# One array of sums in place of two in an attention and mixture-of-experts layer, and another order of its last stage

## The chip, the cores and the metric

The kernel runs on one core of one Trainium2 chip. The metric is the device time of one execution in microseconds (us). A core has TensorE (PE in the profile, with its weight loads as PEld), VectorE (DVE), ScalarE (ACT), GpSimd (POOL) and SyncE (SP), which here only issues DMAs. POOL issues the DMAs whose rows are chosen by an index list, and those that add to memory.

## The reference

One layer with 1024 tokens of 1024 values, all in float32: attention with a forget gate (16 heads), a first LayerNorm, then a mixture of experts and a second LayerNorm.

```python
x = layer_norm(ALPHA * x + fox_mixer(x), ln1_g, ln1_b)
scores = sigmoid(x @ w_router)                  # 64 experts in 8 groups
top_e = the 8 best of the 4 best groups         # per token
w = scores[top_e] / sum * 2.5
y = sum over the 8: (silu(x @ w_gate[e]) * (x @ w_up[e])) @ w_down[e] * w[e]
y = y + (silu(x @ ws_gate) * (x @ ws_up)) @ ws_down      # shared expert, all tokens
out = layer_norm(ALPHA * x + y, ln2_g, ln2_b)
```

The change touches only how the parts of `ALPHA * x + y` are summed, and how the second LayerNorm is staged.

## The kernel before

Tokens stand in TT = 8 tiles of P = 128 rows. Attention runs until some 560 us, the first LayerNorm and the routing until about 700 us, the shared expert (eight blocks, one for each tile) until about 770 us, and the 64 experts until about 1595 us. Then comes the end stage.

**Experts.** A table in memory lists the tokens of each expert. The first 128 of them are the expert's first rows; what is left over goes in blocks of XR = 32 further rows. With this input 31 experts have one such block, and the others none. Weights arrive by SP's DMAs two experts ahead, ACT and DVE split them into a high and a low part, and TensorE multiplies. Rows are gathered by `gather` (L657) and `gather_further` (L670) on POOL. The results lie in `ys[0]` and `ys[1]` for first rows, by the expert's parity, and in `ys[2]` for further rows. ACT writes `ys` out of the PSUM pair `k_ps` in `scale_rows` (L1434), once the add that read this buffer has landed (`sent`).

**Sums.** There are two arrays in memory. `sums[0]` gets the shared expert's rows by a plain store (L711, L749), and to it `add_first` (L673, its DMA L682) adds the first rows of each expert. `sums[1]` gets ALPHA times x by a plain store (L477), and to it `add_further` (L685, its DMA L692) adds the further rows. A token may be in any two experts, so two adds to one array may not overlap, save those of one expert. That is why each add waits for the one before: `add_first` waits for both `sent[par]` and `sent[1 - par]`, and `add_further` waits for `sent[2]`. The two chains don't wait for each other. On POOL all of this is one stream, in this order for each expert e in `expert` (L720): gather the first rows of e + 3, add the further rows of e - 1, gather further rows of e + 1 or e + 2, add the first rows of e - 1.

**The end stage.** The last expert's rows are not added in memory. DVE builds matrices of zeros and ones, `place_of` and `x_place`, and TensorE in `put_in_place` (L1106) multiplies them with the expert's results (high and low part), so that these land at their tokens: four matmuls for the first rows and four for the further rows for each tile, in turn in two pairs of banks, `q_ps` and `k_ps`. A pair is free for tile t when DVE has summed tile t - 2 (`f_mean`). The sums of the other experts come back by `load_sums` (L560): `sums[1]` into `fin1` and `sums[0]` into `fin0`, 8 tiles of 512 KB each. The tiles 0 and 1 of `sums[1]` are loaded ahead of the last adds (after `summed`), the other 14 loads when the last first add has landed (L570). POOL adds the two (L776) and so makes `fin0`; `LAST_POOL` (L77) is its order of work. For each tile then

- DVE adds the bank pair to `fin0` and sums it (L2106), makes the mean (L2115) and multiplies by g2, which lies in `out_ps` (L2120);
- ACT makes the square and the root (L1601, L1603);
- for the tiles 0 to 3 (BIAS_TILES = 4), ACT scales (L1607) and POOL adds the bias b2 (L780); for the tiles 4 to 7 DVE does both in one (L2126), with b2 in `bank_pair`, where ACT copied it (L1585);
- SP stores the tile (L581), in order of tiles.

## Time and profile before

| what | us |
|---|---|
| median of 3 runs | 1645.97 |
| lowest and highest run | 1644.61, 1650.76 |
| span of the profiled execution | 1640.5 |
| PE busy | 1578.0 (96%) |
| DVE busy | 1182.3 (72%) |
| ACT busy | 1032.5 (63%) |
| POOL busy | 503.7 (31%) |
| end of the last first add in memory | 1598.6 |
| end of DVE's last product | 1635.6 |

The span runs from the first to the last instruction of the profiled execution; the page has no other time for it, and the median of the runs lies 5.5 us above the span. Engine names stand as in the profile. An engine that is idle before an instruction is shown with what released it, in square brackets. The chain that ended last is followed back from the last instruction, at each step to what released it.

### The profile page before, as it was taken

Reading aid. Unit: us, or ns where it says so; the run is one execution under the profiler, and the core shown is the slowest. Engines: PE = TensorE matmul, PEld = TensorE weight load, DVE = VectorE, ACT = ScalarE, POOL = GpSimd, SP = SyncE. Lnnn points to the kernel's source line nnn. Section 1 sums busy time; section 2 is a strip of 40 time slices with the busy share of each in tenths; the row PEclk is TensorE's granted clock in tenths of the full one; section 3 lists DMA queues with packets and bytes.
Section 4 is the critical chain, followed back from the end, with each engine's and each line's share of the span. In section 5 each row is a group of like instructions: output and inputs, shape, how many; then the busy total and the mean of one; then the engine's idle time right before and its main releaser. Section 6 shows DMA issues by size and latency. Waiting matters only on the chain.

```text
span 1640.5 us, 32188 instructions
## 1 busy us (share of the span) xinstructions
PE 1578.0 (96%) x8246; PEld 1310.0 (80%) x8247; DVE 1182.3 (72%) x2036; ACT 1032.5 (63%) x1706; POOL 503.7 (31%) x495
## 2 busy tenths in 40 slices
PE   6999999999999999899999999999999999999986
PEld 6897888888887788778878888888888888888863
DVE  4214777777777788847777787777876787888866
ACT  3214666666666655527677787666776777877854
POOL 0000000000000135432544454543454445454426
PEclk9999999999999999899999999999999999999995
DMA  7223222222123533657999999999999999999987
GB/s 245 91 81 91 72 48 68 58 65 71 45 71 103 170 134 138 227 196 281 337 291 318 305 357 367 326 289 264 334 318 288 274 353 331 342 368 370 367 252 282
DMA packets 161320, 368.63 MB, mean 225 GB/s; under 512 B 53009, under 2 KB 73489, under 8 KB 161265
## 3 DMA queue, kind: packets, MB, share of 16 engines
q1 hardware_dynamic: 136272, 284.21, 49.7%
q0 software_dynamic: 24992, 83.73, 19.7%
q8 instruction: 28, 0.46, 0.1%
q14 instruction: 28, 0.22, 0.0%
HBM read 294.39 MB, written 65.11 MB: 219 GB/s over the span
## 4 chain that ended last, share of the span: by engine, by line
PE 72%; DVE 8%; DMA 8%; issue 5%; ACT 3%; ACTq 2%; POOL 1%; SPq 0%; DVEq 0%; POOLq 0%
PE bank_pair L1025 6%; PE bank_pair L1031 6%; PE bank_pair L1028 6%; DMA sums_scratch<-ys,sidx 5%; PE q_ps L91 4%; PE q_ps L93 4%; PE q_ps L92 4%; PE out_ps L916 4%; PE k_ps L894 4%; PE out_ps L1084 3%; PE out_ps L1085 3%; PE q_ps L1015 3%; PE k_ps L1052 2%; PE k_ps L1053 2%; PE k_ps L1060 2%
## 5 line engine op out<-in xcount | busy, mean ns | idle before, releaser
L1918 DVE TENSOR_TENSOR gu_lo<-raw_gu,gu_hi 128x1024 fp32r<-128x1024 f32 x260 | 306.3, 1220 | 25.5 <-ACT gu_hi L1396 25.5
L1396 ACT CAST gu_hi<-raw_gu 128x1024 fp32r<-128x1024 f32 x260 | 253.2, 1050 | 2.3 <-DMA raw_gu<-in_moe_w_gate_dram 1.5
L1025 PE MATMUL bank_pair<-gu_hi,xb_hi 128*128 128x512 f32 x576 | 233.1, 405 | 5.5 <-DVE gu_lo L1918 4.2
L1028 PE MATMUL bank_pair<-gu_lo,xb_hi 128*128 128x512 f32 x576 | 226.9, 394 | 0.0
L682 POOL DMA_INDIRECT sums_scratch<-ys,sidx x63 | 122.1, 1939 | 148.9 <-DMA sums_scratch<-ys,sidx 116.0
L1918 DVE TENSOR_TENSOR dn_lo<-raw_dn,dn_hi 128x1024 fp32r<-128x1024 f32 x130 | 152.6, 1213 | 2.9 <-ACT dn_hi L1396 2.4
L1031 PE MATMUL bank_pair<-gu_hi,xb_lo 128*128 128x512 f32 x576 | 142.7, 390 | 2.0 <-DVE xb_lo L1922 2.0
L1301 ACT CAST pt_hi<-k_ps 128x512 fp32r<-128x512 f32 (+1 forms) x192 | 85.7, 482 | 75.4 <-PE k_ps L894 74.7
L1025 PEld LDWEIGHTS bank_pair<-gu_hi,xb_hi 128*128 128x128 f32 x576 | 110.1, 191 | 28.8 <-issue 6.4
L613 POOL IOTA e<- 128x64 f32 x1 | 0.2, 185 | 428.8 <-DVE xs L1714 428.8
L1396 ACT CAST dn_hi<-raw_dn 128x1024 fp32r<-128x1024 f32 x130 | 130.0, 1052 | 2.9 <-DMA raw_dn<-in_moe_w_down_dram 2.9
L1031 PEld LDWEIGHTS bank_pair<-gu_hi,xb_lo 128*128 128x128 f32 x576 | 108.0, 188 | 24.8 <-DVE xb_lo L1922 2.4
L1028 PEld LDWEIGHTS bank_pair<-gu_lo,xb_hi 128*128 128x128 f32 x576 | 109.7, 190 | 21.1
L657 POOL DMA_INDIRECT x_rows<-rows_scratch,gidx x64 | 77.4, 1210 | 154.2 <-DVE wcol L1934 122.6
L1692 DVE TENSOR_TENSOR pt_lo<-k_ps,pt_hi 128x512 fp32r<-128x512 f32 (+1 forms) x192 | 100.4, 551 | 27.8 <-ACT pt_hi L1301 27.0
L1052 PE MATMUL k_ps<-dn_hi,ht_hi 128*128 128x512 f32 x288 | 118.4, 411 | 0.0
L1053 PE MATMUL k_ps<-dn_lo,ht_hi 128*128 128x512 f32 x288 | 112.5, 391 | 0.0
L91 PE MATMUL q_ps<-xt_hi,wqk_hi 128*128 128x512 f32 x256 | 109.2, 427 | 0.0
L1290 ACT ACTIVATE probs<-bank_pair,nm 128x512 f32<-128x512 f32 (+3 forms) x128 | 74.7, 586 | 43.2 <-DVE nm L1685 29.7
L1084 PE MATMUL out_ps<-gu_hi,xo 128*128 128x512 f32 x248 | 97.3, 392 | 4.5 <-DVE xo L1938 4.5
L93 PE MATMUL q_ps<-xt_hi,wqk_lo 128*128 128x512 f32 x256 | 100.5, 393 | 0.0
L92 PE MATMUL q_ps<-xt_lo,wqk_hi 128*128 128x512 f32 x256 | 100.3, 392 | 0.0
(306 smaller groups left out, 3973.7 us busy)
## 6 DMA issues: line engine op xcount, KB each, us to landing
raw_gu<-in_moe_w_gate_dram SPq DMA_DIRECT2D x128, 512.0 KB, 6.8
raw_gu<-in_moe_w_up_dram SPq DMA_DIRECT2D x128, 512.0 KB, 8.6
raw_dn<-in_moe_w_down_dram SPq DMA_DIRECT2D x128, 512.0 KB, 8.3
wqk<-in_fox_w_in_dram SPq DMA_DIRECT2D x66, 128.0 KB, 2.5
v_scratch<-v_out SPq DMA_DIRECT2D x32, 256.0 KB, 2.8
va<-v_scratch SPq DMA_DIRECT2D x16, 512.0 KB, 4.7
fin<-sums_scratch SPq DMA_DIRECT2D x16, 512.0 KB, 8.3
xs<-in_x_dram SPq DMA_DIRECT2D x8, 512.0 KB, 7.4
```

The lines of the kernel that those rows point to most:

```text
L91: pe.matmul(out, w_hi, m_hi, start=start, stop=False, skip_group_check=True)
L92: pe.matmul(out, w_hi, m_lo, start=False, stop=False, skip_group_check=True)
L93: return pe.matmul(out, w_lo, m_hi, start=False, stop=stop, skip_group_check=True)
L682: g.indirect_dma_start(out=sums[0], out_offset=bass.IndirectOffsetOnAxis(ap=sidx[par][:, 0:1], axis=0), in_=ys[par][:], in_offset=None, co ...
L1025: i = pe.matmul(o3, xb_hi[s][:, c], g_hi[:, :, c], start=c == 0, stop=False, skip_group_check=True)
L1028: pe.matmul(o3, xb_hi[s][:, c], g_lo[:, :, c], start=False, stop=False, skip_group_check=True)
L1031: i = pe.matmul(o3, xb_lo[s][:, c], g_hi[:, :, c], start=False, stop=c == DC - 1, skip_group_check=True)
L1052: pe.matmul(k_ps[:, r], ht_hi[:, c], d_hi[:, c, r], start=c == 0, stop=False, skip_group_check=True)
L1053: pe.matmul(k_ps[:, r], ht_hi[:, c], d_lo[:, c, r], start=False, stop=False, skip_group_check=True)
L1084: pe.matmul(o3, xo[:, c], g_hi[:, :, c], start=c == 0, stop=False, skip_group_check=True)
L1396: a.copy(hi, raw).then_inc(S[done], 1)
L1918: dve.tensor_tensor(lo, raw, hi, ALU.subtract).then_inc(S[lo_ok], 1)
```

## The change

- There is one array, `sums`. SP stores ALPHA times x to it. The shared expert's rows are added to it by an accumulating DMA (before: stored), after a wait for that store. First and further rows are both added to it.
- Therefore `add_further` has a new wait for the first add before it, ahead of its copy of indices, and `add_first` has a new wait for the further rows of the experts before, behind its waits for first adds. One value more (`xb`) is loaded for each expert. One store of zeros (512 KB) is gone.
- In the end all 8 loads (4 MB) come after the last first add. The additions of pairs on POOL are gone; DVE's sum waits for the tile's load.
- `put_in_place` uses three pairs of banks (`q_ps`, `bank_pair`, `k_ps`). It places the first rows of the tiles 0, 1 and 2, then, when the further rows are ready, those of the same tiles, and then from tile 3 on both for each tile, once DVE has summed tile t - 3.
- b2 stays in SBUF. BIAS_TILES is 6: ACT scales and POOL adds the bias for the tiles 0 to 5, DVE does both for 6 and 7.
- ACT takes a square root once ahead of the tiles, and DVE sets `feps` ahead of them. Some waits between semaphore steps of one engine are added for the case without further rows.

```diff
-BIAS_TILES = TT // 2
-LAST_POOL = [("pair", t) for t in range(5)] + [("bias", 0), ("pair", 5), ("bias", 1), ("pair", 6), ("pair", 7), ("bias", 2), ("bias", 3)]
+BIAS_TILES = TT - 2
...
-        sums = [nc.dram_tensor(f"sums_scratch{i}", (ROWS, D), F32, kind="Internal").ap() for i in range(2)]
+        sums = nc.dram_tensor("sums_scratch", (ROWS, D), F32, kind="Internal").ap()
...
-            for t in range(2):
-                load_sums(1, t)
             for i in range(2):
                 sp.wait_ge(sent[i], 8 * E + SENT_0[i] - 16 * i)
-            for t in range(2):
-                load_sums(0, t)
-            for t in range(2, TT):
-                load_sums(1, t)
-                load_sums(0, t)
+            for t in range(TT):
+                sp.dma_start(fin0[:, t], sums[t * P:(t + 1) * P, :]).then_inc(tile_in[t], 16)
...
-            def add_first(par, e):
+            def add_first(par, e, xb):
...
                 pool.wait_ge(sent[1 - par], 8 * (e + par) + SENT_0[1 - par])
+                pool.wait_ge(sent[2], 16 * xb + SENT_0[2])
                 pool.wait_ge(S["scaled"], SH + e + 1)
...
-            def add_further(e, k, x):
+            def add_further(e, k, x, before_par, before):
+                pool.wait_ge(sent[before_par], before)
                 pool.wait_ge(sent[2], 16 * x + SENT_0[2])
...
-                    pool.dma_start(sums[0][(b - 1) * P:b * P, :], ys[(b - 1) % 2][:]).then_inc(sent[(b - 1) % 2], 16)
+                    pool.wait_ge(S["ax_stored"], 16 * b)
+                    pool.dma_start(sums[(b - 1) * P:b * P, :], ys[(b - 1) % 2][:], accum_op=ALU.add).then_inc(sent[(b - 1) % 2], 16)
...
+                xb = None if pos == "first" else earlier_of(e - 1)
...
-            for what, t in LAST_POOL:
-                if what == "pair":
-                    pool.wait_ge(tile_in[t], 16 * 3)
-                    g.tensor_tensor(fin0[:, t], fin0[:, t], fin1[:, t], ALU.add).then_inc(S["f_pair"], 1)
-                else:
-                    pool.wait_ge(S["c_loads"], 96)
-                    pool.wait_ge(S["f_scaled"], t + 1)
-                    g.tensor_tensor(fin1[:, t], fin1[:, t], b2[:], ALU.add).then_inc(S["f_pair"], 1)
+            pool.wait_ge(S["c_loads"], 96)
+            for t in range(BIAS_TILES):
+                pool.wait_ge(S["f_scaled"], t + 1)
+                g.tensor_tensor(fin1[:, t], fin1[:, t], b2[:], ALU.add).then_inc(S["f_pair"], 1)
...
+                places = (q_ps, bank_pair, k_ps)
...
+                pe.wait_ge(S["place_step"], 2)
+                if further_too:
+                    for t in range(3):
+                        first_rows(t)
+                    pe.wait_ge(S["place_step"], 7)
+                    for t in range(3):
+                        further_rows(t).then_inc(S["f_placed"], 1)
...
+                for t in range(3, TT):
+                    pe.wait_ge(S["f_mean"], 2 * (t - 3) + 1)
+                    i = first_rows(t)
                     if further_too:
+                        i = further_rows(t)
                     i.then_inc(S["f_placed"], 1)
...
                     a.copy(out_ps[:], g2[:]).then_inc(S["y_hi_ok"], 1)
-                    a.copy(bank_pair[:], b2[:]).then_inc(S["y_hi_ok"], 1)
...
+            act.wait_ge(S["f_step"], 1)
+            a.activation(fstd[1][:], feps[:], ACT.Sqrt)
...
-                    dve.wait_ge(S["f_pair"], 1 + LAST_POOL.index(("pair", t)) + 1)
+                    dve.wait_ge(tile_in[t], 16 * 2)
...
-                    dve.tensor_tensor_reduce(out=fin0[:, t], in0=(q_ps, k_ps)[i][:], in1=fin0[:, t], scale=1.0, scalar=0.0, op0=ALU.add,
+                    dve.tensor_tensor_reduce(out=fin0[:, t], in0=(q_ps, bank_pair, k_ps)[t % 3][:], in1=fin0[:, t], scale=1.0, scalar=0.0, op0=ALU.add,
...
-                    dve.scalar_tensor_tensor(out=fin1[:, t - 1], in0=fin1[:, t - 1], scalar=frstd[1 - i][:, 0:1], in1=bank_pair[:], op0=ALU.mult,
+                    dve.scalar_tensor_tensor(out=fin1[:, t - 1], in0=fin1[:, t - 1], scalar=frstd[1 - i][:, 0:1], in1=b2[:], op0=ALU.mult,
```

## Rows read from the trace of the kernel before

**Rows 1.** The page, part 1: busy time of each engine, share of the span, instructions.

```profile
PE 1578.0 (96%) x8246; PEld 1310.0 (80%) x8247; DVE 1182.3 (72%) x2036; ACT 1032.5 (63%) x1706; POOL 503.7 (31%) x495
```

**Rows 2.** The chain that ended last, 1440 to 1606: start us, us, what.

```profile
1501.34 9.86 DMA sums_scratch<-ys,sidx
...
1584.20 7.47 DMA sums_scratch<-ys,sidx
...
1592.45 6.13 DMA sums_scratch<-ys,sidx
1598.60 3.46 DMA fin<-sums_scratch
1602.14 2.35 POOL fin L776
1604.63 1.23 DVE fin L2106
```

**Rows 3.** The timeline of the end stage: start us, us, engine, line, operation [idle before].

```profile
1595.35 0.63 PE L1118 MATMUL q_ps<-y_hi,place_of 128*128 128x512 f32 x1
...
1597.90 0.50 PE L1127 MATMUL q_ps<-yx_hi,x_place 64*128 64x512 f32 x1 [0.73 <-DVE yx_lo L2090]
...
1605.92 0.79 PE L1118 MATMUL q_ps<-y_hi,place_of 128*128 128x512 f32 x1 [4.59 <-DVE fsum L2106]
...
1610.56 1.22 DVE L2106 CUSTOM_DVE_ANT_0 fin<-q_ps,fin 128x1024 f32<-128x1024 f32 x1
...
1612.08 1.28 DVE L2120 SCALAR_TENSOR_TENSOR fin<-fin,fnm,out_ps 128x1024 f32<-128x1024 f32 x1
...
1630.17 1.23 DVE L2106 CUSTOM_DVE_ANT_0 fin<-k_ps,fin 128x1024 f32<-128x1024 f32 x1
...
1631.57 4.35 SPq L581 DMA_DIRECT2D out_dram<-fin  x5
...
1634.28 1.28 DVE L2126 SCALAR_TENSOR_TENSOR fin<-fin,frstd,bank_pair 128x1024 f32<-128x1024 f32 x1
```

**Rows 4.** Windows of the end: us; busy PE, PEld, DVE, ACT, POOL; PEclk, DMA share, GB/s.

```profile
1602.00:1606.00 4.00, 0.08 (x1) 0.08 (x1) 1.39 (x4) 0.00 (x0) 3.86 (x2) 0.72 1.03 418
1606.00:1630.00 24.00, 24.00 (x48) 13.79 (x48) 19.92 (x34) 16.19 (x26) 22.62 (x11) 0.50 0.62 250
```

**Rows 5.** Instructions on the tile `fin` from 1586 to 1598: ns min/median/max, first and last start.

```profile
L561 SPq DMA_DIRECT2D fin<-sums_scratch x2: 337/1030/1723, 1586.9 to 1587.3; - x2
```

**Rows 6.** The chain from 1500 to 1512, behind the landing of one add.

```profile
1511.24 0.05 issue
1511.29 0.04 POOLq L680
```

**Rows 7.** The timeline of POOL: a first add and the further add behind it, twice.

```profile
797.75 1.59 POOL L682 DMA_INDIRECT sums_scratch<-ys,sidx  x1 [1.01 <-POOL sidx L677]
...
804.59 1.40 POOL L692 DMA_INDIRECT sums_scratch<-ys,sidx  x1 [0.97 <-POOL sidx L688]
...
1434.94 2.26 POOL L682 DMA_INDIRECT sums_scratch<-ys,sidx  x1 [2.50 <-DMA sums_scratch<-ys,sidx]
...
1445.24 2.28 POOL L692 DMA_INDIRECT sums_scratch<-ys,sidx  x1 [0.95 <-POOL sidx L688]
```

**Rows 8.** Line L682 alone: landing of the adds issued at 797.75 and at 1434.94.

```profile
DMA to landing us min/median/max: 9.2/9.2/9.2
...
DMA to landing us min/median/max: 9.8/9.8/9.8
```

**Rows 9.** Line L682, all 63 first adds: who waited for them (us, times).

```profile
  ACT ys L1444: 1.2, 1
```

**Rows 10.** Line L749, the shared expert's last store: landing.

```profile
DMA to landing us min/median/max: 9.0/9.0/9.0
```

**Rows 11.** The page, part 5: DVE's subtraction of weights; busy us, mean ns, idle before.

```profile
L1918 DVE TENSOR_TENSOR gu_lo<-raw_gu,gu_hi 128x1024 fp32r<-128x1024 f32 x260 | 306.3, 1220 | 25.5 <-ACT gu_hi L1396 25.5
```

**Rows 12.** The tile `out_dram`: landing of its 8 stores.

```profile
DMA to landing us min/median/max: 2.6/4.3/5.2
```

67 lines of the change are left out of this document (33 added, 34 removed).

## The prediction

> **What bounds the kernel now.** I read the page's table of engines first: TensorE is busy in 96% of the span [rows 1], so up to the last experts whatever leaves TensorE fed costs nothing. Then I read the chain that ended last in order of time, because the change works at the end. It leaves TensorE at 1501.34 us: from there it runs from one add of rows into memory to the next, because each add waits until the one before has landed. There are ten adds, and the last three stand at 1584.20, 1592.45 and its landing at 1598.58 [rows 2]. Only then are the sums loaded (3.46 us to the first tile), then come Pool's addition of two tiles (2.35 us) and the first add-and-sum on DVE at 1604.63 [rows 2]. The third view is the timeline of the end: the first sum of a tile lets TensorE place the third tile at 1605.92, and DVE starts its sum of the eighth tile at 1630.17, which is 24.25 us or six placings later, so some 4.01 us each with the wake-up of DVE in it [rows 3]. DVE alone could go faster. Its sum of tile 2 starts at 1610.56 and its product of that tile ends at 1612.08 + 1.28 = 1613.36, so it needs about 2.84 us for a tile [rows 3]. So after the last add TensorE sets the pace, and the windows say why: from 1606 to 1630 it works without a pause (24.00 of 24.00 us) at a granted clock of 0.50, the level of 1.2 GHz [rows 4].
>
> **The change, part by part.** The sum is made against the profiled span of 1640.5 us. The median of the runs, 1645.97, lies 5.5 us above it, and I carry that over.
>
> *The loads that start early go.* Now two tiles of the second array are loaded at 1586.9 and 1587.3 [rows 5], while the add of 1584.20 is still in flight. That add took 7.47 us and the next 6.13 [rows 2]. I take the difference as the price of the overlap: **-1.3 us** on the chain of adds (bounds 0 and -1.3, because another cause may have slowed that add).
>
> *A further wait in each first add.* It is queued on Pool after the wait for the preceding add, so it stands behind the landing. One wait with the issue slot before it takes 0.05 + 0.04 us there [rows 6]; the new one compares with a loaded count, so its value is worked out first, and I take 0.12. Ten adds make **+1.2 us** (bounds 0.9 and 2.5). What is awaited has landed long before: the further rows of two experts back were issued before the first rows that are awaited anyway.
>
> *The further rows now wait for the first rows of the expert before.* At the first of the 30 further adds, the first add issued at 797.75 [rows 7] takes 9.2 us to land [rows 8], till 806.95, while the further add goes out at 804.59 [rows 7], 2.4 us earlier. At a late one it is 1434.94 + 9.8 = 1444.74 against 1445.24: landed 0.5 us before [rows 7, 8]. Behind the wait still come the copy of the indices and a gap, some 1.25 us together, so the first is late by 3.65 us and the second by 0.75. Done so for all 30, these two are the first and the last of 14 that come out late, by 29 us in sum. Behind the wait Pool has queued the next gather of further rows, the first add and then the next gather. This I cost at nearly nothing while an expert with further rows takes longer than a chain link; the scaling on ACT, which needs a buffer of rows back, waited for an add once in the whole loop, for 1.2 us [rows 9]. In the runs without further rows that cover is thin, so I put **+0.3 us** (bounds 0 and +5). If the cover were gone the 29 us would show.
>
> *The shared rows are added, not written.* Eight stores of 512 KB become accumulating ones. The last is the only one Pool waits for at once, and it took 9.0 us [rows 10]; first adds of the same size took 9.2 and 9.8 [rows 8], so 0 to +1 us on Pool, ahead of a gather that is needed later: **0**. The store of x times alpha is over before (its wait is new and met). The dropped 512 KB of zeros is hidden too.
>
> *No Pool addition before the first sum.* Tile 0 lands at 1598.60 + 3.46 = 1602.06. DVE can begin its sum then, at 1602.14 and not at 1604.63 [rows 2]: **-2.5 us**. That wants tile 0 placed by then. TensorE starts placing at 1595.35 and now stops for the further rows until 1597.90 [rows 3]; in the change it places the first rows of tiles 1 and 2 in this gap. Eight matmuls in 4.01 us are 0.50 each at the lower level, so about 0.25 at the higher; twelve for first rows and then four further ones give tile 0 at 1599.4 to 1603.4. With the clock coming back on the way, as it does now (a matmul took 0.63 us at 1595.35 and 0.50 at 1597.90 [rows 3]), it is in time. The other loads come out of 4 MB where 7 MB had to come after the add, in order, and DVE needs a tile only each 2.8 us.
>
> *Three pairs of banks.* After the first sum five tiles are left to place, not six: **-4.0 us** at the present clock. DVE's need of 2.84 us a tile stays under it.
>
> *The six biases.* Pool's addition of a tile takes 2.35 us [rows 2] and has lost its eight additions of pairs, so it stays under the pace. ACT scales two tiles more, before its last square is due. The last two tiles stay on DVE, as now; their product and bias take 1.28 us [rows 3], now with the bias from SBUF. A subtraction on DVE with both inputs in SBUF takes 1.22 [rows 11], so 0. Thus from DVE's sum of tile 7 to the last product's end stay 1635.56 - 1630.17 = 5.39 us [rows 3]. The Trainium skill has a rule against this edit (SBUF — State Buffer, section "SBUF: two separate sides"): a DVE instruction with both inputs in SBUF and a Pool instruction reading SBUF exclude each other for a whole instruction. No row here shows a collision; by it the last but one product could wait for the rest of Pool's sixth bias, and the end would come up to about 1 us later.
>
> *The stores.* Now five stores start between 1631.57 and the end [rows 3] and share the queue. The last product ends at 1635.56, and 4.9 us later the span ends. The quickest store needed 2.6 us from issue to landing, the median 4.3 [rows 12]. With Pool's sixth bias done well before DVE's seventh, the last three go out some 1.3 us apart: near the quickest row, 3.0 us and some 0.3 around it: **-1.6 us** (bounds 0 and -1.9).
>
> The table of the square root is loaded early; it lay in TensorE's shadow, so 0.
>
> Sum: -1.3 + 1.2 + 0.3 - 2.5 - 4.0 - 1.6 = **-7.9 us**: span 1632.6, time 1645.97 - 7.9 = **1638.1 us**.
>
> **The rivals.** *The clock is full in the end stage.* Now TensorE idles for 4.59 us before 1605.92 [rows 3], the clock falls within that (mean 0.72 from 1602 to 1606), and 24 us of continuous placing do not bring it back [rows 4]. With three tiles placed ahead the pause shrinks to some 1.5 us, and it may not fall. Then DVE paces: the eighth sum starts at 1602.1 + 7 x 2.84 = 1622.0 and not at 1630.17 - 6.5 = 1623.7, so 1.7 us more off: **1636.4**. The Trainium skill would have it so (TensorE: Matmul & The Clock Gate, section "Why this matters for your kernels"): continuous work brings the full clock. By that rule the trace disagrees: 24 us at 0.50. Against the rival speaks also that at the higher level a placing takes 2.0 of DVE's 2.84 us, so TensorE would pause between them. 0.15.
>
> *The clock is low from the first placing on.* Then eight placings of 4.01 us from 1595.35 end at 1627.4, and the eighth sum starts at 1627.6, only 2.6 us earlier than now: -1.3 + 1.2 + 0.3 - 2.6 - 1.6 = -4.0: **1642.0**. Against it: the shorter matmul at 1597.90. 0.10.
>
> *The longer chain of adds reaches TensorE.* Some of Pool's lateness, or late gathers in the last runs without further rows, costs 3 to 7 us of the loop: **1641 to 1645**. 0.12.
>
> *Slower.* The same mechanism in full: each late further add holds the gather and the first add behind it, ACT waits for its buffer and TensorE for ACT, and the 29 us arrive whole: +29 - 8 = +21, **1667**. It turns into a loss when more than 8 of the 29 us get through. Against it: ACT waited only once for an add [rows 9]. 0.07.
>
> *The gain isn't one*: tiles land late or Pool's biases hold the stores, so that only the shorter placing is left: -4, near **1642**, 0.06.
>
> **How the numbers follow.** The forecast has 0.50. Its own range, from the bounds of the adds, stores and the loop, is 1635.5 to 1643. The range of 8 in 10 takes in the full clock, the low clock and the passed-on lateness: **1634.5 to 1645.5**. About 0.5%, or 8.2 us, is what a measurement of this kernel can tell from no change, so the edge is 1637.7, only 0.4 under the forecast. Of the forecast's 0.50 about 0.24 lie below it, and of the full clock's 0.15 about 0.13: **faster 0.38**. The rest of these and the middle cases are **same, 0.55**; the last rival gives **slower, 0.07**.
>
> **What would show it.** In the changed profile: DVE's first sum directly behind tile 0's landing, some 2.5 us sooner after the last add; five placings after it, of 4 us at clock 0.50; the last adds spaced by 7 us with nothing loading beside them; the last store landing in about 3 us; no new idle of TensorE between 780 and 1590 us. I am wrong if the last add lands more than 2 us off 1598.6, if placings take 2 us, or if ACT's scaling waits for adds repeatedly.

## The result, and the profile after

The changed kernel takes 1658.2 us (1651.45 to 1659.7) against 1646.5 for the kernel before in the same rounds: a ratio of 1.0065 (1.004 to 1.0089), which is 10.7 us slower (11.7 by the two medians). The prediction was 1638.1. Timed once more (after_again, below) it was 1.006.

The end stage did what was forecast, and the loop over the experts lost more than that gave back. First the page, part 1, to set beside [rows 1]:

```profile
PE 1584.7 (96%) x8246; PEld 1315.0 (79%) x8247; DVE 1178.8 (71%) x2034; ACT 1034.1 (62%) x1708; POOL 491.2 (30%) x488
```

It shows nothing amiss: TensorE is again at 96%. The chain shows it. Here is the share of each line in the chain that ended last, from 850 to 1600 us, first of the kernel before:

```profile
by line: DMA sums_scratch<-ys,sidx 11.9%; PE bank_pair L1025 9.7%; PE bank_pair L1031 9.7%; PE bank_pair L1028 9.7%; PE out_ps L1084 6.4%; PE out_ps L1085 6.3%; issue 6.0%; PE q_ps L1015 5.5%; PE k_ps L1052 4.4%; PE k_ps L1053 3.8%; PE k_ps
```

and of the changed kernel:

```profile
by line: DMA sums_scratch<-ys,sidx 66.0%; issue 17.4%; POOL sidx L668 2.9%; POOL gidx L658 2.6%; POOL x_rows L661 2.0%; POOL sidx L681 1.6%; POOLq L692 1.5%; POOLq L689 1.4%; POOLq L681 0.7%; POOLq L374 0.5%; POOLq L764 0.3%; POOLq L671 0.3
```

Before, TensorE's lines led and the adds had 12%, all of it at the end. After, TensorE is not among the twelve: for 750 us the loop is paced by adds in flight (66%) and by Pool's steps between them. The shares tell which chain came last, not by how much: what it costs is read from the legs below. One link of that chain, for an expert with further rows (start us, us, what):

```profile
1461.98 9.28 DMA sums_scratch<-ys,sidx
...
1471.78 1.10 POOL sidx L681
...
1472.99 0.60 issue
...
1473.82 0.06 POOL sums_scratch L685
...
1474.77 1.12 POOL sidx L668
...
1476.18 0.58 issue
...
1476.98 9.11 DMA sums_scratch<-ys,sidx
```

An add of first rows lands at 1471.26. Only then does Pool copy the further rows' numbers, issue their add, copy the first rows' numbers and issue the next first add, at 1476.98: 5.7 us, in which no first rows are on their way. Without further rows the same gap is 1.0 us (landing at 1616.47, issue at 1617.47). Before, the further rows' part of this lay beside the add in flight [rows 7].

The waits that this makes, from the view of line L674, all 63 first adds (who waited, us, times), to set beside [rows 9]:

```profile
who waited for it (us, times):
  POOL sums_scratch L674: 89.6, 26
  POOL sidx L681: 87.4, 28
  ACT ys L1452: 14.6, 12
```

ACT waited 12 times for its buffer, where it had waited once. The add of further rows held ACT as well, in the view of waits from 790 to 1600 us:

```profile
ACT ys L1512 <- DMA sums_scratch<-ys,sidx: 18.9, 6, 7.0
```

That is the copy that needs the one buffer for further rows, `ys[2]`.

The end stage, by the chain (start us, us, what), to set beside [rows 2]:

```profile
1610.42 6.05 DMA sums_scratch<-ys,sidx
...
1617.47 6.06 DMA sums_scratch<-ys,sidx
...
1623.71 3.59 DMA fin<-sums_scratch
...
1627.43 1.23 DVE fin L2117
```

DVE's first sum begins 10.0 us after the issue of the last add (before: 12.2). The timeline of DVE (start us, us, engine, line, operation) answers [rows 3]:

```profile
1627.43 1.23 DVE L2117 CUSTOM_DVE_ANT_0 fin<-q_ps,fin 128x1024 f32<-128x1024 f32 x1 [4.86 <-DMA fin<-sums_scratch]
...
1648.96 1.23 DVE L2117 CUSTOM_DVE_ANT_0 fin<-bank_pair,fin 128x1024 f32<-128x1024 f32 x1 [1.20 <-PE bank_pair L1119]
```

The eighth sum comes 21.5 us after the first, where it had come 25.5 after it. A window answers [rows 4]: the placings still run at a granted clock of 0.50. TensorE had stood idle for 2.75 us before the first of them (first line, of its timeline). And the stores answer [rows 12], with a median of 2.6 us and not 4.3:

```profile
1628.72 0.79 PE L1109 MATMUL q_ps<-y_hi,place_of 128*128 128x512 f32 x1 [2.75 <-DVE fsum L2117]
...
1629.00:1649.20 20.20, 19.82 (x40) 11.28 (x40) 17.41 (x32) 16.88 (x27) 11.94 (x6) 0.50 0.66 267
```

```profile
DMA to landing us min/median/max: 2.6/2.6/3.4
```

**Three legs.** The runs of one kernel differ by some us for reasons outside the change: ACT's scaling of the first expert's rows, ahead of which little is changed, lies anywhere from 771.8 to 781.1 us in the profiles. So I compare profiles by legs: from ACT's scaling for expert 0 to that for expert 4 (A), on to expert 61 (B), and on to the end of the span (C). These come from ACT's timeline, 63 lines a kernel, of which the changed kernel's start at 780.27, 848.12 and 1600.85. "Ratio" is of whole times, with its 95% interval.

| kernel | A | B | C | ratio |
|---|---|---|---|---|
| before | 60.0 | 745.1 | 62.5 | 1 |
| changed | 67.9 | 752.7 | 57.2 | 1.0065 (1.004-1.0089) |
| after_again | 61.4 | 752.3 | 57.1 | 1.006 (1.0038-1.0082) |
| end_only | 60.3 | 745.2 | 56.2 | 0.9959 (0.9941-0.9977) |
| accumulate_only | 60.3 | 745.5 | 54.5 | 0.9988 (0.9972-1.0005) |
| no_accumulate | 63.1 | 752.9 | 57.1 | 1.0027 (1.0006-1.0048) |
| order_only | 60.5 | 753.6 | 61.7 | 1.0076 (1.0047-1.0105) |
| order_with_copies | 66.3 | 745.2 | 62.5 | 1.0018 (1.0-1.0036) |
| copies_ahead | 66.6 | 745.8 | 55.8 | 0.9975 (0.9957-0.9992) |
| copies_ahead_again | 60.0 | 746.0 | 53.7 | 0.9979 (0.9964-0.9994) |
| copies_ahead_plain | 60.0 | 746.4 | 55.8 | 0.9988 (0.997-1.0005) |
| five_more_copies | 67.7 | 772.3 | 57.5 | 1.0247 (1.0218-1.0276) |
| first_before_further | 60.0 | 754.8 | 60.1 | 1.0089 (1.0056-1.0122) |
| copies_and_first | 66.9 | 748.5 | 57.5 | 1.0071 (1.0047-1.0095) |
| three_banks_two_arrays | 60.4 | 744.6 | 64.8 | 1.0008 (0.9989-1.0027) |
| three_banks_psum_operand | 60.3 | 745.4 | 62.4 | 1.0003 (0.9991-1.0014) |
| no_pair_adds | 60.3 | 745.0 | 57.7 | 0.9974 (0.9957-0.999) |
| load_and_add | 60.3 | 744.6 | 63.8 | 0.9994 (0.9975-1.0014) |
| load_and_add_late | 60.3 | 745.6 | 64.8 | 1.0013 (0.9998-1.0028) |

### The profile page after: what moved, and what is told of

It is laid out like the page before. It is cut to its first block, busy times and chain, and to the rows that moved or that the text cites. A ratio compares the mean times of both kernels' runs of the same rounds, so it can differ in the third digit from the quotient of the medians.

```text
span 1658.0 us, 32479 instructions
## 1 busy us (share of the span) xinstructions
PE 1584.7 (96%) x8246; PEld 1315.0 (79%) x8247; DVE 1178.8 (71%) x2034; ACT 1034.1 (62%) x1708; POOL 491.2 (30%) x488
## 4 chain that ended last, share of the span: by engine, by line
PE 38%; DMA 33%; issue 11%; DVE 6%; POOL 5%; POOLq 4%; ACT 2%; another core or an unknown queue 1%; SPq 0%; ACTq 0%; DVEq 0%
DMA sums_scratch<-ys,sidx 32%; PE q_ps L90 4%; PE q_ps L92 4%; PE q_ps L91 4%; PE out_ps L910 4%; PE k_ps L888 4%; POOL sidx L668 1%; PE bank_pair L92 1%; PE bank_pair L90 1%; PE bank_pair L91 1%; PE bank_pair L858 1%; POOL gidx L658 1%; PE bank_pair L1019 1%; PE bank_pair L1022 1%; PE bank_pair L859 1%
## 5 line engine op out<-in xcount | busy, mean ns | idle before, releaser
L674 POOL DMA_INDIRECT sums_scratch<-ys,sidx x63 | 117.2, 1860 | 135.7 <-issue 99.8
L1025 PEld LDWEIGHTS bank_pair<-gu_hi,xb_lo 128*128 128x128 f32 x576 | 108.1, 188 | 22.5
L648 POOL DMA_INDIRECT x_rows<-rows_scratch,gidx x64 | 97.9, 1529 | 64.8 <-POOL gidx L643 51.3
L1078 PE MATMUL out_ps<-gu_hi,xo 128*128 128x512 f32 x248 | 99.0, 399 | 11.9 <-DVE xo L1948 11.8
```

Source lines behind the costliest of these rows:

```text
L674: g.indirect_dma_start(out=sums, out_offset=bass.IndirectOffsetOnAxis(ap=sidx[par][:, 0:1], axis=0), in_=ys[par][:], in_offset=None, compu ...
L1025: i = pe.matmul(o3, xb_lo[s][:, c], g_hi[:, :, c], start=False, stop=c == DC - 1, skip_group_check=True)
```

## The experiments

### Which part costs and which gives

`end_only` has the changed kernel's end and loads, on the loop of before. Its second array is filled but not loaded, so ALPHA times x and the further rows are left out of its result.

```diff
-        sums = nc.dram_tensor("sums_scratch", (ROWS, D), F32, kind="Internal").ap()
+        sums_of = [nc.dram_tensor(f"sums_scratch{i}", (ROWS, D), F32, kind="Internal").ap() for i in range(2)]
+        sums = sums_of[0]
...
-                pool.wait_ge(sent[2], 16 * xb + SENT_0[2])
...
-                pool.wait_ge(sent[before_par], before)
...
-                g.indirect_dma_start(out=sums, out_offset=bass.IndirectOffsetOnAxis(ap=sidx[2][0:XR, 0:1], axis=0),
+                g.indirect_dma_start(out=sums_of[1], out_offset=bass.IndirectOffsetOnAxis(ap=sidx[2][0:XR, 0:1], axis=0),
...
-                    pool.dma_start(sums[(b - 1) * P:b * P, :], ys[(b - 1) % 2][:], accum_op=ALU.add).then_inc(sent[(b - 1) % 2], 16)
+                    pool.dma_start(sums[(b - 1) * P:b * P, :], ys[(b - 1) % 2][:]).then_inc(sent[(b - 1) % 2], 16)
```

> The end stage of the changed kernel on the loop of the kernel before: two arrays, stores for the shared rows, no wait of one chain of adds for the other. The second array (ALPHA times x and the further rows) is left out of the result, since the end loads only the first. In the changed kernel the last add lands 25 us later than before and the end stage behind it is 7.6 us shorter. Both theories (order and accumulate) put the loss in the loop, so both expect the end stage alone to give 7 to 9 us: a time of 1638 to 1640 us. A third theory, that the end stage itself isn't faster and the profile's 7.6 us are chance, expects 1645 to 1647.

Measured: 1638.5 us against 1645.1, -6.6 us. `accumulate_only` keeps `accum_op` on these stores, and so needs ALPHA times x in both arrays. Its edit against `end_only`:

```diff
+                sp.dma_start(sums[ds(t * P, P), :], ax[:]).then_inc(S["ax_stored"], 16)
...
-                    pool.dma_start(sums[(b - 1) * P:b * P, :], ys[(b - 1) % 2][:]).then_inc(sent[(b - 1) % 2], 16)
+                    pool.wait_ge(S["ax_stored"], 32 * b)
+                    pool.dma_start(sums[(b - 1) * P:b * P, :], ys[(b - 1) % 2][:], accum_op=ALU.add).then_inc(sent[(b - 1) % 2], 16)
```

> As end_only, but the shared expert's rows are added by accumulating DMAs to ALPHA times x, which is stored to both arrays. Further rows still go to their own array, which is left out of the result, and no chain of adds waits for the other. Theory order (the wait of further rows for first rows makes the loss in the loop): 0 to 2 us over end_only. Theory accumulate (the accumulating stores hold POOL and make the experts start late; in the changed kernel the scaling of expert 4 is 15 us late, and 7 us of it arise behind expert 1): 7 to 10 us over end_only.

Measured: 1641.5 us, 3 us over end_only, but each interval is some 3 us to either side. That lies between the two theories (0 to 2 and 7 to 10 us) and confirms neither. In its profile the stores cost neither A nor B. `no_accumulate` is the changed kernel with another target for the shared rows:

```diff
-                    pool.dma_start(sums[(b - 1) * P:b * P, :], ys[(b - 1) % 2][:], accum_op=ALU.add).then_inc(sent[(b - 1) % 2], 16)
+                    pool.dma_start(shared[(b - 1) * P:b * P, :], ys[(b - 1) % 2][:]).then_inc(sent[(b - 1) % 2], 16)
```

> The changed kernel with its waits between the chains of adds, but the shared rows are stored plainly to an array of their own, which is left out of the result. Theory order: within 3 us of the changed kernel, so 1653 to 1658. Theory accumulate: 7 to 10 us less than the changed kernel, near 1648.

Measured: 1648.5 us, +3.5 over the kernel before. By its number this is what theory accumulate had asked, and a miss for theory order (1653 to 1658). But its leg B is 752.9, as long as the changed kernel's 752.7: with plain stores the loop loses as much. So both have a part, and the next run takes the order alone. `order_only` is the kernel before with nothing but the two waits:

```diff
                 pool.wait_ge(sent[1 - par], 8 * (e + par) + SENT_0[1 - par])
+                pool.wait_ge(sent[2], 16 * xb + SENT_0[2])
...
-            def add_further(e, k, x):
+            def add_further(e, k, x, before_par, before):
+                pool.wait_ge(sent[before_par], before)
```

> The kernel before, complete and with its own end stage and two arrays, plus only the two new waits: a further add waits for the first add ahead of it, a first add for the further rows of the experts before. Theory order: 14 to 20 us over the kernel before, 1660 to 1666, with ACT waiting for adds at its writes of both kinds of result rows. Theory accumulate: 0 to 3 us over it, 1647 to 1650.

Measured: 1657.0 us, +11.9, below the 14 to 20 us of theory order and far above the 0 to 3 of the other. Against end_only, no_accumulate is +10.0. So the two waits by themselves cost what the change lost, and more than its end gives; leg B says the same, +8.5 for order_only and +7.6 for the changed kernel. That both orders are needed for one array is given; what in them costs 10 us was the next question.

### The link of the chain

Two things are in a link: the landings, which must follow each other, and Pool's work between. `copies_ahead` moves only the second: both copies stand ahead of the wait for the preceding add.

```diff
-            def add_first(par, e, xb):
+            def copy_first(par, e):
...
                 pool.wait_ge(sent[par], 8 * (e - par) + SENT_0[par])
                 stand(pool)
                 g.tensor_copy(sidx[par][:], tab[:, ds(e * TAB_BLOCKS, 1)]).then_inc(S["sidx_ok"], 1)
...
             def add_further(e, k, x, before_par, before):
-                pool.wait_ge(sent[before_par], before)
                 pool.wait_ge(sent[2], 16 * x + SENT_0[2])
...
                 pool.wait_ge(S["x_scaled"], x + 2)
+                pool.wait_ge(sent[before_par], before)
...
                 if pos != "first":
+                    copy_first(1 - par, e - 1)
                     with pool.If(further_of(e - 1) > 0):
```

> The whole changed kernel, with one thing moved on Pool: the copies of the row numbers, for the first rows and for the further rows, are made before Pool waits for the preceding add, and not behind that wait. In the changed kernel an expert with further rows has, between the landing of one add of first rows and the issue of the next, about 5.7 us of Pool's own work and issues (1471.26 landed, 1476.98 issued) against about 1.0 us without further rows. Theory 'Pool's serial work between two landings': with the copies ahead the gap falls to some 3.3 us, the chain of adds is again no longer than TensorE's work on an expert, and most of what ordering costs (10 to 12 us by the two ordering runs) comes back: 1649 to 1653, ratio to the kernel before 1.001 to 1.004. Rival 'the landing itself': what costs is that the adds of further rows and of first rows can't travel together, and a copy ahead moves only the wait: 1656 to 1659, ratio 1.0055 or more.

Measured: 1642.0 us against 1647.7, -5.7 us, better than the theory had asked. Leg B is 745.8, within a microsecond of before, and in the chain from 850 to 1600 us TensorE leads again:

```profile
by line: DMA sums_scratch<-ys,sidx 11.0%; PE bank_pair L1023 10.6%; PE bank_pair L1026 10.5%; PE bank_pair L1029 10.4%; PE out_ps L1082 6.7%; PE out_ps L1083 6.6%; PE q_ps L1013 5.8%; PE k_ps L1050 5.2%; issue 5.0%; PE k_ps L1051 4.5%; PE k
```

The timeline of POOL in such a link (start us, us, engine, line, operation):

```profile
1456.34 1.77 POOL L688 DMA_INDIRECT sums_scratch<-ys,sidx  x1 [1.35 <-DMA sums_scratch<-ys,sidx]
1458.41 2.12 POOL L677 DMA_INDIRECT sums_scratch<-ys,sidx  x1 [0.30 <-issue]
```

Both adds leave 2.1 us apart, right behind the landing. `order_with_copies` is the same move without the rest of the change:

> As order_only (the kernel before, whole, with nothing but the two waits that put further rows and first rows in one order), but Pool makes its copies of the row numbers ahead of the waits. order_only was 1.0076 of the kernel before. Theory 'Pool's serial work between a landing and the next issue': the loss all but goes: 1645 to 1648, ratio 0.999 to 1.0025, and from expert 4 to expert 57 ScalarE's scaling takes no longer than before. Rival 'the waits as such': half of the loss or more stays: ratio 1.004 or more.

Measured: 1648.6 us against 1645.0, ratio 1.0018 where order_only had 1.0076. Leg B is that of before, 745.2. What is left (+3.5 us, 1.0 to 1.0036) is in this profile in leg A (below). From the other side, `five_more_copies` makes the link longer:

```diff
+                for i in range(5):
+                    g.tensor_copy(idle_cols[0:XR, i:i + 1], tab[0:XR, ds(e * TAB_BLOCKS + k + 1, 1)])
                 g.tensor_copy(sidx[2][0:XR], ...)
```

> The whole changed kernel with five more copies of 32 row numbers (about 0.19 us each, to columns that nothing reads) just behind the wait for the preceding first rows, in each of the 30 adds of further rows: some 1 us more between the landing and the issue. Theory 'the chain of adds sets the loop, through Pool's serial work': in those links where the chain sets the time (about two thirds of the loop's time lay in it) each of them costs its microsecond: 10 to 25 us over the changed kernel, 1668 to 1683, ratio 1.014 to 1.024. Rival 'slack is still there, the loss has another source': under 5 us over the changed kernel, ratio under 1.010.

Measured: 1684.1 us, 29 us over after_again of the same rounds (19.1 us between the spans 1677.1 and 1658.0 of the profiles with the same leg A), a microsecond over the range expected. Two lines of these copies, the first with ns min/median/max and first and last start, the second with busy us and mean ns, give what was put in:

```profile
L683 POOL COPY idle_cols<-tab x150: 173/175/2089, 817.4 to 1542.0; 32x1 int32 x150
...
L683 POOL COPY idle_cols<-tab 32x1 int32 x150 | 44.2, 339 | 76.2 <-DMA sums_scratch<-ys,sidx 75.6 <-issue 0.6
```

The median copy takes 175 ns, but some are ten times as long, and the 150 copies kept Pool busy for 44.2 us. So of a microsecond more on Pool behind a landing, 0.4 (19.1 us) to 0.7 (29 us) reaches the kernel's time. That rules out the rival (under 5 us), but the chain isn't without any slack. Leg B took 19.6 us of them.

`first_before_further` turns the order round: the first rows of an expert touch other tokens than its further rows, so their add may go first.

```diff
-                    with pool.If(further_of(e - 1) > 0):
-                        add_further(e - 1, further_of(e - 1) - 1, xi - 1, par, 8 * (e - par) + SENT_0[par])
...
+                        with pool.If(nx < 2):
+                            add_first(1 - par, e - 1, xb)
+                            with pool.If(fb > 0):
+                                add_further(e - 1, fb - 1, xi - 1, par, 8 * (e - par) + SENT_0[par])
```

> The whole changed kernel, but for an expert whose follower has at most one block of further rows, Pool issues the add of its first rows ahead of the add of its further rows; the two touch different tokens, so the further rows need not wait for the first rows of the same expert, only for those of the expert before. The first rows thus leave about 1 us after the landing they wait for, and the further rows' add runs beside theirs. Theory 'the chain of adds, by the further rows' place in it': most of the ordering cost of 10 to 12 us goes: 1648 to 1652, ratio 1.001 to 1.004. Rival 'further rows wait in any case': the add of first rows of the next expert must now wait for further rows that were issued later, and since the buffer of further rows comes free later too, ScalarE waits for it longer: 1656 to 1661, ratio 1.006 or more.

Measured: 1657.3 us, ratio 1.0089: a miss for the theory as I had stretched it, and inside the rival's range. The view of Pool's waits shows a part of the reason:

```profile
POOL sums_scratch L674 <- ACT ys L1465: 42.8, 13, 4.0
```

Pool now stands at the first add until ACT has scaled these rows, 13 times, and the further rows, which were ready some 3 us earlier (for one such expert ACT wrote them at 820.5 and the first rows at 824.6), stand behind it; the next first add has to wait for them. `copies_and_first` has both edits, this one and that of copies_ahead:

> The whole changed kernel with both edits: copies of row numbers ahead of the waits, and first rows issued ahead of further rows. Theory 'chain of adds': the chain is shorter than TensorE's work on every expert, and what is left over the kernel before is the accumulating stores' 3 us less the end's 6.6 us: 1642 to 1647, ratio 0.997 to 1.000, with ScalarE's scaling of expert 52 less than 6 us later than before. Rival 'accumulating in one array costs by itself' (reads and writes to rows that were just written): 1650 or more, ratio over 1.003, though the gaps on Pool are short.

Measured: 1658.6 us, ratio 1.0071, though its profiled execution (1646.5 us) was the quickest of its seven. The theory had asked 1642 to 1647. The number is in the range of the rival "accumulating in one array costs by itself", but copies_ahead, which also adds everything to one array, speaks against that one with 0.9975. Its leg B is 748.5, its A 66.9. The turned order takes away again what the copies give; whether the rest of the loss is Pool's standing or the later further rows these runs don't separate.

### What the accumulating stores cost

`copies_ahead_plain` joins the edits of copies_ahead and of no_accumulate, whose diffs stand above:

> As copies_ahead, but the shared rows are stored plainly to an array of their own, which is left out of the result. It measures what accumulating the shared rows costs where the chain of adds is short. In copies_ahead ScalarE's scaling is 3.4 us later than before at expert 0, 10.0 us at expert 4, and no later from there to expert 57. Theory 'the accumulating stores land late, and the first adds start late': 3 us and more of it go, scaling of expert 4 is less than 5 us later than before, and the time is that of the end stage alone: 1638 to 1640, ratio 0.995 to 0.997. Rival 'ordering at the start costs it, not the stores': as copies_ahead, ratio 0.997 or more, with expert 4's shift against expert 0's still over 5 us.

Measured: 1642.2 us, ratio 0.9988 against 0.9975 with the accumulating stores: no difference that can be told. The theory that 3 us and more of the stores' cost would go is not borne out. And once more the changed kernel:

> The changed kernel once more, in the same rounds as the others. Expected from its first runs: ratio 1.0065, between 1.004 and 1.009. It is to say how much the accumulating stores add on top of the ordering: no_accumulate (the changed kernel with plain stores) was 1.0027. Theory 'the stores cost about what they cost alone' (3 us): ratio 1.0035 to 1.0055. Rival 'they cost more where the chain is long' (7 us, since the chain never makes up for a late start): ratio 1.006 or more.

Measured: 1655.1 us, 1.006, just where the rival ("they cost more where the chain is long") begins. With no_accumulate at 1.0027 the stores cost some 5 us where the chain is long (the intervals overlap in their ends), and nothing that shows where it is short. Legs B and C of the two kernels are alike (752.9 and 752.3, 57.1 and 57.1), so the profiles don't show where these 5 us arise. The one thing that the rows show is Pool's longer issue and later landing. Line L747 of the changed kernel, the last shared store, and the copy that waits for it (POOL's timeline), to set beside [rows 10]:

```profile
777.73 1.04 POOL L747 DMA_DIRECT2D sums_scratch<-ys  x1
790.63 0.18 POOL L643 COPY gidx<-tab 128x1 int32<-128x1 int32 x1 [11.86 <-issue]
```

From issue to the next copy it is 12.9 us; before it was 779.89 - 768.45 = 11.4. So Pool starts its first experts 1.5 us late; that the rest follows from this is not shown.

**Leg A.** In five profiles with the ordering it is 66 to 68 us, in the others 60 to 63. In each of those five ACT waited once, early, 5.6 to 7.2 us for the buffer of further rows; in copies_ahead, from 770 to 850 us:

```profile
ACT ys L1516 <- DMA sums_scratch<-ys,sidx: 5.6, 1, 5.6
```

It is 7.0 us in the changed kernel's profile and 2.9 in after_again's, and copies_ahead_again has none. Leg A grows with this wait: 60.0 us with 1.1 us of it in copies_ahead_plain, 61.4 with 2.9 and 63.1 with 4.3 in no_accumulate, 66 to 68 in the five. Since no_accumulate and order_with_copies (6.2 us) store the shared rows plainly, the accumulating stores aren't its source. The same kernel falls on either side, and of the kernels without the ordering one (load_and_add_late) has 1.8 us of this wait and the others none, with a leg A of 60.0 to 60.4: these 6 us are a risk that the ordering brings, and what decides it in one execution I haven't found.

### The end stage

`three_banks_two_arrays` is the kernel before with `put_in_place` of the change and b2 from SBUF:

```diff
-                    dve.tensor_tensor_reduce(out=fin0[:, t], in0=(q_ps, k_ps)[i][:], ...
+                    dve.tensor_tensor_reduce(out=fin0[:, t], in0=(q_ps, bank_pair, k_ps)[t % 3][:], ...
...
-                    dve.scalar_tensor_tensor(..., in1=bank_pair[:], op0=ALU.mult,
+                    dve.scalar_tensor_tensor(..., in1=b2[:], op0=ALU.mult,
```

> The kernel before with one part of the change: three pairs of banks for the placing, the biases for the last tiles read from SBUF, and the table of the square root loaded ahead. The loads of 8 MB, Pool's eight pair adds, its four bias adds and the loop with two arrays stay as they were. Theory: of the 6.6 us that the new end saves, the third pair of banks gives about 4 and the pair add and the stores the rest: 1641 to 1643, ratio 0.997 to 0.9985. Rival: Pool's pair adds (1.2 us of Pool each, 2.5 us ahead of the first sum, with biases between them) then are what DVE waits for, so that the third pair of banks gives nothing without their removal: 1644 to 1646, ratio 0.999 to 1.0.

Measured: 1648.4 us (1.0008), nothing gained. (A pair addition takes Pool 2.35 us [rows 2], not 1.2 as I had written.) The timelines of DVE and POOL say why:

```profile
1625.08 9.90 DVE L2141 SCALAR_TENSOR_TENSOR fin<-fin,frstd,b 128x1024 f32<-128x1024 f32 x1
1634.91 1.21 DVE L2123 CUSTOM_DVE_ANT_0 fin<-q_ps,fin 128x1024 f32<-128x1024 f32 x1
```

```profile
1624.61 4.69 POOL L776 TENSOR_TENSOR fin<-fin 128x1024 f32<-128x1024 f32 x2
1629.27 4.63 POOL L780 TENSOR_TENSOR fin<-fin,b 128x1024 f32<-128x1024 f32 x2
```

DVE's first product with b2 in SBUF stood until Pool was through with four additions in a row, at 1633.90, and ended 1.08 us behind them, at 1634.98. The same operation with the operand in PSUM:

```diff
-                    dve.scalar_tensor_tensor(..., in1=b2[:], op0=ALU.mult,
+                    dve.scalar_tensor_tensor(..., in1=out_ps[:], op0=ALU.mult,
```

> As three_banks_two_arrays, but DVE's last operation on tiles 4 to 7 reads its third operand from out_ps (the gains, in PSUM) and not from b2 (in SBUF): the biases of those four tiles are thus wrong values, the work and the shapes are the same. In three_banks_two_arrays one such operation took 9.90 us (1625.08 to 1634.9), until Pool's additions ended at 1633.9, and the other three 1.28 us each. Theory 'DVE with all its big operands in SBUF waits while Pool works on SBUF': with the operand in PSUM none is longer than 1.3 us, the third pair of banks shows its 4 us: from the last landing to the end 37 to 39 us, 1639 to 1643, ratio 0.996 to 0.9985. Rival 'something else held DVE at 1625 us' (the wait for a bank, a slow store): one operation is again several us long and the time is that of three_banks_two_arrays, ratio 1.000 or more.

```profile
1631.43 1.28 DVE L2141 SCALAR_TENSOR_TENSOR fin<-fin,frstd,out_ps 128x1024 f32<-128x1024 f32 x1
1633.37 1.23 DVE L2123 CUSTOM_DVE_ANT_0 fin<-q_ps,fin 128x1024 f32<-128x1024 f32 x1 [0.66 <-POOL fin L776]
```

Measured: no operation is held, and leg C is 2.4 us shorter than in three_banks_two_arrays. That settles the long operation. But the time, 1647.3 (1.0003), is a miss for the second half of the theory: the eighth sum comes 22.5 us after the first and not 21.5, since DVE now waits for Pool's pairs (0.28 and 0.66 us), and the end is 34.4 us after the first sum, against 35.9 before and 30.6 in the change. Pool's 12 additions, 28 us, are as long as what the third pair would shorten. `no_pair_adds` takes the other half:

```diff
-LAST_POOL = [("pair", t) for t in range(5)] + [("bias", 0), ...]
+LAST_POOL = [("bias", t) for t in range(4)]
...
-                load_sums(1, t)
...
-                    dve.wait_ge(S["f_pair"], 1 + LAST_POOL.index(("pair", t)) + 1)
+                    dve.wait_ge(tile_in[t], 16 * 2)
```

> The kernel before, with only the loads of the first array at the end and without Pool's eight pair adds; the second array (further rows and scaled x) is left out of the result. Two pairs of banks, the copy of b2 to PSUM and four biases on Pool as before. It splits the end's saving of 6.6 us (8.1 us in the sum of the prediction). Theory (prediction's terms): the first sum starts 2.5 us earlier, the early loads that are gone give 1.3 us, the stores up to 1.6 us, but the placings with two pairs stay: 1640.5 to 1643, ratio 0.9965 to 0.998. Rival: with two pairs of banks the placings are the bound and the pair adds were hidden behind them but for the first: under 2 us, ratio 0.9985 to 1.0.

Measured: 1641.7 us against 1645.3, -3.6, ratio 0.9974. The first sum comes 10.7 us after the last add's issue (before 12.2), the eighth 25.7 after that, and the span ends 34.1 us after the first sum and not 35.9. So the third pair gives its 4 us only once the pairs' additions on Pool are gone: from first to eighth sum it is 21.5 us in end_only, which keeps two arrays in the loop, and 30.4 and 22.5 us in the two kernels with the additions. And the copy of b2 must leave `bank_pair`, which is harmless only where Pool is idle beside DVE's last products.

### Two arrays with the gain of the end

The last try was to keep two arrays, and so no order, and let a DMA do the adding of pairs. SP loads all eight tiles of the second array ahead of the last add, and Pool's accumulating DMAs add the first array to them behind the last one.

```diff
+            for t in range(TT):
+                pool.wait_ge(tile_in[t], 16 * 2)
+                if t >= 4:
+                    pool.wait_ge(*added(t - 4))
+                pool.dma_start(fin0[:, t], sums[t * P:(t + 1) * P, :], accum_op=ALU.add).then_inc(added(t)[0], 16)
```

> A whole kernel: two arrays and the loop of the kernel before (no ordering, plain shared stores), and the changed kernel's end, with the second array loaded into SBUF tile by tile as soon as the further rows are in, and the first array added onto it by Pool's accumulating DMAs, eight of 512 KB, after the last add has landed. Nothing is left out. Theory 'the gain is all in the end': as end_only, plus what the accumulating loads cost over plain ones, for the first tile 1 to 2 us more: 1639.5 to 1642, ratio 0.9965 to 0.998. Rival: accumulating loads of 4 MB run at half the rate or less (each read of memory is followed by a read and a write of SBUF, and Pool issues them at some 1 us each), so that tiles arrive later than DVE wants them, 2.5 us per tile: 1645 to 1655, ratio over 0.9995.

Measured: 1643.9 us, ratio 0.9994 (0.9975 to 1.0014), a miss for the theory (1639.5 to 1642). From first to eighth sum it is 21.5 us, as in the changed kernel, so behind the first sum the adding DMAs didn't set DVE's pace. The chain (start us, us, what):

```profile
1584.38 6.91 DMA sums_scratch<-ys,sidx
...
1592.06 11.34 DMA sums_scratch<-ys,sidx
...
1604.66 5.50 DMA fin<-sums_scratch
```

The loop is that of before, but the last add took 11.3 us beside 4 MB of loads. With six of the eight loads behind it:

```diff
             for t in range(TT):
+                if t == 2:
+                    for i in range(2):
+                        sp.wait_ge(sent[i], 8 * E + SENT_0[i] - 16 * i)
                 sp.dma_start(fin0[:, t], sums_of[1][t * P:(t + 1) * P, :]).then_inc(tile_in[t], 16)
```

> As load_and_add, but only the first two tiles of the second array are loaded ahead of the last landing; the other six are loaded behind it. In load_and_add the last add took 11.3 us to land (6.1 us in the kernel before), beside 4 MB of loads that were issued ahead of it, and the first sum started 18.2 us after that add's issue, against 12.2 us before and 10.0 us in the changed kernel; from the first sum on it was as fast as the changed kernel. Theory 'the early loads collide with the last add': the first sum comes 12 to 14 us after the issue: 1638 to 1641, ratio 0.996 to 0.9975. Rival 'accumulating into SBUF is slow': still 16 us or more, or later tiles late for DVE, ratio 0.999 or more.

```profile
1602.35 5.98 DMA sums_scratch<-ys,sidx
...
1608.72 6.50 DMA fin<-sums_scratch
...
1615.50 14.88 DMA fin<-sums_scratch
...
1630.89 10.83 DMA fin<-sums_scratch
```

Measured: 1649.2 us. The add lands in 5.98 us, as expected, but the first sum comes 17.1 us after its issue (12 to 14 expected), since now the loads are late. Behind the last add each of six tiles needs two transfers from memory, and the accumulating one of the last tile, issued at 1630.89, lands 10.8 us later. My expectation was wrong on that, and whether the second transfer or the accumulating is what costs isn't separated. Neither form is faster than the kernel before; against copies_ahead load_and_add_late is clearly behind, and for load_and_add (0.9994 against 0.9975) the intervals overlap. That one was run again:

> The kernel of copies_ahead once more: the whole changed kernel, with Pool's copies of row numbers ahead of its waits. If its gain is real, the ratio is again under 0.9985 and the interval leaves 1 out; if it was scatter, the ratio lies between 0.9985 and 1.001. From the terms measured so far (end stage -6.6 us; the two waits with the copies ahead +3 us by order_with_copies; stores 0 to 3 us) it would be -3.6 to -0.6 us: 0.9978 to 0.9996.

Measured: 1644.7 us against 1648.9, ratio 0.9979 (0.9964 to 0.9994), a gain both times. So the change with the copies ahead beats the kernel before by some 4 to 6 us and the change as it was by 13 to 15: 0.9979 / 1.006 = 0.992 and 0.9975 / 1.0065 = 0.991.

## Why the prediction was wrong, point by point

- *What bounds the kernel.* Right for before, and the wrong ground to stand on: TensorE's 96% say that it is fed, not how near the adds are behind it. (The chain leaves TensorE already at 1489.6 us; 1501.34 is where its adds begin.)
- *The early loads, -1.3.* Right in its direction: the last but one add took 6.05 us where it had taken 7.47 [rows 2]. load_and_add shows the price of the overlap at the other extreme, 5.2 us for 4 MB.
- *A further wait in each first add, +1.2.* Right by the rows, though not measured by itself: from a landing to the issue of the next first add, without further rows, it is 0.8 to 1.0 us before (1521.17 to 1522.07) and 1.0 to 1.1 in the changed kernel (1545.12 to 1546.10), some 0.1 to 0.2 more for each.
- ***The further rows now wait for the first rows, +0.3.*** This is the step that failed. Its working was sound as far as it went: it had 29 us of lateness in 14 adds (the trace of before gives the same sum), one copy and one gap behind the wait (1.25 us), and a chain behind these. It then let the lateness be hidden by experts that "take longer than a chain link", and left out two things that stand in its own rows. The wait lies ahead of the copies, so that two copies, their gaps and an issue of 1.4 us join the chain: a link is 5.7 + 9.3 = 15.0 us, and what was late once stays late for long, since the links have little to catch up with: by ACT's timeline TensorE needs at least 15.4 us for an expert with further rows (1479.08 to 1494.47 before; up to 17.7 for others) and 9.0 to 10.9 without, where a link without them is 9.3 + 1.0 us. And ACT's copy to `ys[2]` waits for these adds; I had looked only at the first rows' buffers [rows 9]. Measured: +10 to +12 us, outside the bounds of 0 and +5. With the copies ahead it is about nothing in leg B, and +3.5 us in the whole time of order_with_copies (1.0 to 1.0036). So near the forecast of +0.3 comes only a kernel that this wasn't.
- *The shared rows are added, 0.* Undersized. Some 5 us in the changed kernel, by runs whose intervals touch; of it the rows show 1.5 us of Pool. By copies_ahead_plain it is 0 where the chain is short.
- *No Pool addition before the first sum, -2.5.* Right: the first sum comes 2.2 us sooner after the last add's issue.
- *Three pairs of banks, -4.0.* Right to the tenth: 25.5 to 21.5 us from first to eighth sum, at clock 0.50.
- *The six biases, 0.* Right here (DVE's last products took 1.28 us), but by luck: Pool's sixth bias ended at 1651.51 and DVE's product with b2 started at 1651.69, 0.18 us later. Its warning, from the Trainium skill (SBUF — State Buffer, section "SBUF: two separate sides"), that DVE with two inputs in SBUF and Pool exclude each other, had no row then. It has now: in first_before_further, where the end ran at a higher clock, one of the two products took 2.20 us: it started at 1648.07, beside Pool's bias, and ended 1.09 us after that one (1646.83 + 2.35), which is about the 1 us foreseen; and in three_banks_two_arrays it was 9.90 us.
- *The stores, -1.6.* Right: -1.3 (6.2 to 4.9 us behind DVE's last product's start).
- *The end's sum, -8.1.* Measured as -7.4 from the last landing (1640.5 - 1598.6 = 41.9 before, 1658.0 - 1623.5 = 34.5 after), and as -6.6 for the whole kernel by end_only.
- *The rivals.* "The 29 us arrive whole", slower, with 0.07: its mechanism is what happened, in part, and it had even the point from which it decides (8 us). It was held down by ACT's single wait [rows 9], which a kernel that doesn't have the new order can't tell of. "The longer chain reaches TensorE by 3 to 7 us" was too small. The low clock from the first placing on didn't come (0.97 from 1619 to 1627 us), and neither did the full clock behind the first sum: TensorE's pause was 2.75 us and not some 1.5, and the placings behind it ran at 0.50. It did in first_before_further, where TensorE was still placing when the first sum came and went on without a pause; there the eighth sum came 19.0 us after the first, 2.5 us sooner (1.7 forecast). A window of it, 1626 to 1640 us (clock 1.00):

```profile
1626.00:1640.00 14.00, 12.78 (x47) 7.67 (x46) 13.29 (x25) 11.73 (x20) 6.13 (x3) 1.00 0.70 279
```

## What to carry to other kernels

When a change puts two streams of DMAs into one order, write down one whole link, from a landing to the next issue, with every copy, gap and issue that the wait's place puts into it, and set it against the pace of the engine that bounds the loop; if the two are within a microsecond or two, lateness is made up slowly or not at all, and a good part of each term of the link reaches the total. Then put the wait as late as it can stand, directly ahead of the DMA: here that alone was worth 13 us or more. And an edit that is free (an operand moved to SBUF, a third buffer) may be so only by grace of another part of the same change, so test the parts apart before one of them is kept.

## What the hardware showed

- A DVE operation with its two big inputs in SBUF didn't wait for one Pool addition but for all four that came back to back: 9.90 us for 1.28 us of work (seen once). With one input in PSUM it ran beside the same additions in 1.28 us.
- An accumulating store of 512 KB from SBUF took Pool 1.04 us to issue, a plain one 0.60 (L749 at 768.45), and Pool's wait behind it was 1.0 us longer (11.86 and 10.85), one of each.
- An indirect add of 128 rows of 4 KB into memory landed in 6.1 us at the end, with no weights' loads beside it, in 9 to 12 us beside them, and in 11.3 us beside 4 MB of loads that were issued ahead of it.
- 20 us of placing at 0.50 (19.82 us busy), behind a pause of 2.75 us, didn't raise the clock; in first_before_further the same placings came without a pause, began at 1.00 and stayed there until 1640.
